# Smaller expert blocks in two mixture-of-experts layers: 48 rows in place of 64, and 22 overflow blocks in place of 16

## What is computed

```python
def hier_moe(h, w_grp, b_grp, w_rt, b_rt, w_up, w_down):
    g_gate, g_idx = top_k(softmax(xt @ w_grp + b_grp), 1)      # one of 4 groups
    e_val, e_idx = top_k(the 8 logits of that group, 2)        # two experts of it
    gate = softmax(e_val) * g_gate
    expert = g_idx * 8 + e_idx                                 # 2 of 32 experts for each token
    for each expert e, its rows x:
        a, u = split(x @ w_up[e], 2)                           # w_up[e]   1024 x 1024
        y = (silu(a) * u) @ w_down[e]                          # w_down[e]  512 x 1024
    return the sum over a token's two experts of gate * y
h = h + hier_moe(...)        # output: h without the 16 learned tokens
```

```
18 21 22 31 22 33 18 39 | 25 40 28 36 12 14 22 31
38 30 54 42 47 42 54 53 | 27 41 25 33 25 31 39 31
```

## Time and profile before

| | |
|---|---|
| median of 3 runs | 2815.74 us |
| profiled execution, its own time | 2807.85 us |
| its span | 2806.0 us |
| TensorE busy | 2567.0 us (91%) |
| weight loads into TensorE | 1356.2 us (48%) |
| VectorE, ScalarE, GpSimd busy | 875.4, 568.4, 480.3 us |
| HBM read and written | 507.26 MB, 23.10 MB |

### The profile page before, as it was taken

One profiled execution on the slowest core, in us unless ns is written; L12 is line 12 of the kernel. 1 busy time (PEld: TensorE's weight loads), 2 busy tenths in 40 slices (PEclk: granted clock), 3 DMA queues, 4 the chain that ended last, 5 costly groups with the idle time before them and its releaser, 6 DMA issues. The chain is left out here.

```text
span 2806.0 us, 37484 instructions
## 1 busy us (share of the span) xinstructions
PE 2567.0 (91%) x15258; PEld 1356.2 (48%) x15258; DVE 875.4 (31%) x1809; ACT 568.4 (20%) x1341; POOL 480.3 (17%) x682
## 2 busy tenths in 40 slices
PE   7997898988989999889999999959999899989985
PEld 4654444435554454555555555434455454444442
DVE  2306512353251221664111211120556542111112
ACT  2106112232221111631000010021345111000000
POOL 2623210071231121340000000020344200000001
PEclk9998999997999999999999999979999899999997
DMA  5211013110021420125999999951001089999997
GB/s 177 85 66 46 30 35 120 42 41 2 4 77 37 144 90 32 38 77 209 358 411 411 411 411 411 369 193 53 32 32 61 1 337 411 411 411 411 411 411 282
DMA packets 180273, 532.33 MB, mean 190 GB/s; under 512 B 21360, under 2 KB 31472, under 8 KB 180144
## 3 DMA queue, kind: packets, MB, share of 16 engines
q1 hardware_dynamic: 167536, 505.22, 46.5%
q10 hardware_dynamic: 10240, 16.79, 1.6%
q0 software_dynamic: 2368, 8.52, 0.9%
HBM read 507.26 MB, written 23.10 MB: 189 GB/s over the span
## 5 line engine op out<-in xcount | busy, mean ns | idle before, releaser
L344 PE MATMUL psum<-weight_ring,hidden_T 128*128 128x512 f32 (+2 forms) x1216 | 475.9, 548 | 2.7 <-PEq L576 1.6
L344 PEld LDWEIGHTS psum<-weight_ring,hidden_T 128*128 128x128 f32 x1216 | 228.7, 191 | 223.0 <-issue 158.2
L2982 PE MATMUL psum<-arena,hidden_T 128*64 128x512 f32 x1344 | 296.2, 592 | 0.0
L2971 PEld LDWEIGHTS psum<-hidden_T,arena 128*128 128x128 f32 x2304 | 266.8, 192 | 49.6 <-issue 49.6
L2971 PE MATMUL psum<-hidden_T,arena 128*128 128x128 f32 x2304 | 283.3, 278 | 0.0
L2994 PE MATMUL psum<-weight_ring,hidden_T 128*64 128x512 f32 x1024 | 235.4, 602 | 34.1 <-DMA weight_ring<-in_moe_w_down 30.0
L3248 POOL DMA_INDIRECT arena<-expert_rows_out,arena x18 | 20.4, 1133 | 1061.9 <-issue 534.3
L2982 PEld LDWEIGHTS psum<-arena,hidden_T 128*64 128x64 f32 x1344 | 100.5, 137 | 186.9 <-issue 186.9
L2982 PE MATMUL psum<-weight_ring,hidden_T 128*64 128x512 f32 x704 | 155.0, 592 | 0.0
L2994 PEld LDWEIGHTS psum<-weight_ring,hidden_T 128*64 128x64 f32 x1024 | 71.0, 137 | 153.0 <-issue 128.5
L2976 DVE TENSOR_TENSOR hidden_T<-psum,norm_gains 128x512 f32<-128x512 f32 x64 | 44.3, 691 | 293.9 <-PE psum L2982 182.7
(11 more groups left out here) (546 smaller groups left out, 3195.5 us busy)
## 6 DMA issues: line engine op xcount, KB each, us to landing
arena<-in_moe_w_up SPq DMA_DIRECT2D x84, 2048.0 KB, 24.1
weight_ring<-in_moe_w_down SPq DMA_DIRECT2D x64, 2048.0 KB, 24.0
weight_ring<-in_moe_w_up SPq DMA_DIRECT2D x44, 2048.0 KB, 23.4
weight_ring<-in_hg_w_in SPq DMA_DIRECT2D x8, 2048.0 KB, 10.6
weight_ring<-in_ev_w_in SPq DMA_DIRECT2D x8, 1536.0 KB, 6.9
weight_ring<-in_fox_w_in SPq DMA_DIRECT2D x6, 2048.0 KB, 8.1
weight_ring<-in_od_w_in SPq DMA_DIRECT2D x5, 2048.0 KB, 8.0
weight_ring<-in_ple_w_gate SPq DMA_DIRECT2D x4, 2048.0 KB, 9.3
```

Source lines behind the costliest of these rows:

```text
L344: last = nc.tensor.matmul(out, l, r, start=i == 0, stop=i == len(left) - 1)
L2971: last = nc.tensor.matmul(g.psum[:, c // 4, (c % 4) * P:(c % 4 + 1) * P], keep[:, i, c * P:(c + 1) * P], row[:, i, :], start=i == 0, stop= ...
L2982: last = nc.tensor.matmul(g.psum[64 * q:64 * q + 64, 2 + n, :].rearrange("p (s c) -> p s c", s=2), xT[:, k // 4, k % 4, ROWS * n:ROWS * n ...
```

## The change

Each expert's own block has 48 rows, a pair's slots are 96, and there are 22 overflow blocks of 48 rows. What follows from it: the 0/1 matrices, the moving side of `pick` and the copies of `place` have 96 columns for 128; the two stores of a result have 48 rows for 64; the block counts are taken against 10 multiples of 48 instead of 8 of 64; the table of overflow blocks is made with 22 x 32 comparisons instead of 16 x 32; the overflow loop goes around 22 times when there is any block. The products with w_up and w_down keep 64 columns of their stationary side. For the second expert of a pair that reaches 16 columns beyond the 96, so VectorE sets these to zero once per layer, with a wait, ahead of the first `place`. A scratch table moves to another buffer. The one DMA that zeroes the overflow rows early in the program covers 1056 rows instead of 1024.

```diff
-ROWS = 64
-OVER = 16
+ROWS = 48
+PAIR = 2 * ROWS
+OVER = 22
+BLOCKS = 11
@@ host_constants
-    c["steps"] = np.tile(ROWS * np.arange(1, 9, dtype=np.float64), (P, 1))
+    c["steps"] = np.tile(ROWS * np.arange(1, BLOCKS, dtype=np.float64), (P, 1))
@@ zero_expert_rows
-    rows = g.a["y_rows"][NEXP * ROWS:].rearrange("(p n) (two c) -> p (n two) c", p=P, c=512)
+    rows = g.a["y_rows"][NEXP * ROWS:].rearrange("(p n) (two c) -> p (n two) c", p=PAIR, c=512)
@@ stage_route
-            TT(bg, cnt.unsqueeze(2).to_broadcast([P, NEXP, 8]), g.c("steps")...
+            TT(bg, cnt.unsqueeze(2).to_broadcast([P, NEXP, BLOCKS - 1]), g.c("steps")...
@@ stage_experts
-    numbers = g.c("slots").unsqueeze(1).to_broadcast([P, T, P])
+    numbers = g.c("slots")[:, 0:PAIR].unsqueeze(1).to_broadcast([P, T, PAIR])
@@ pick
-                last = nc.tensor.matmul(g.psum[:, c // 4, (c % 4) * P:(c % 4 + 1) * P], keep[:, i, c * P:(c + 1) * P], row[:, i, :], ...
+                last = nc.tensor.matmul(g.psum[:, c // 4, (c % 4) * P:(c % 4) * P + PAIR], keep[:, i, c * P:(c + 1) * P], row[:, i, :], ...
@@ tensor_up
-                last = nc.tensor.matmul(..., xT[:, k // 4, k % 4, ROWS * n:ROWS * n + ROWS], wv[:, k, q, :, :], ...
+                last = nc.tensor.matmul(..., xT[:, k // 4, k % 4, ROWS * n:ROWS * n + 64], wv[:, k, q, :, :], ...
@@ store
-        a = eng.dma_start(rows[:, 0:512], y[n][0:64, :])
-        b = eng.dma_start(rows[:, 512:], y[n][64:128, :])
+        a = eng.dma_start(rows[:, 0:512], y[n][0:ROWS, :])
+        b = eng.dma_start(rows[:, 512:], y[n][64:64 + ROWS, :])
@@ VectorE in stage_experts
             gates_and_overflow(dve, late)
+            nc.vector.memset(xT[:, :, :, PAIR:PAIR + 16], 0.0).then_inc(*late.up())
+            dve.wait_ge(*late.last())
             for n in range(2):
                 dve.wait_ge(turned[n].sem, turned[n].base + 1)
                 place(n).then_inc(placed[n].sem, 1)
```

More of the change, by code:

```diff
@@ L322, in zero_expert_rows @@
     zeros = g.small[:, 512:1024].unsqueeze(1)
-    rows = g.a["y_rows"][NEXP * ROWS:].rearrange("(p n) (two c) -> p (n two) c", p=P, c=512)
-    sp.dma_start(rows, zeros.to_broadcast([P, OVER * ROWS // P * 2, 512])).then_inc(*g.y_rows_zeroed.up(16))
+    rows = g.a["y_rows"][NEXP * ROWS:].rearrange("(p n) (two c) -> p (n two) c", p=PAIR, c=512)
+    sp.dma_start(rows, zeros[0:PAIR].to_broadcast([PAIR, OVER * ROWS // PAIR * 2, 512])).then_inc(*g.y_rows_zeroed.up(16))
 def inverse_root(g, pool, out, sums, scale, chain, done, times=None):
@@ L2679, in stage_route @@
     ovb, inc, base, obase = (g.take(NEXP) for _ in range(4))
-    big = turned_logits.rearrange("p t n -> p (t n)")[:, 0:OVER * NEXP]
+    big = g.hT.rearrange("p k t -> p (k t)")[:, 2 * len(TILES) * NEXP:(2 * len(TILES) + OVER) * NEXP]
     t1 = g.hT.rearrange("p k t -> p (k t)")[:, 0:2 * T * NEXP].rearrange("p (a t e) -> p a t e", a=2, t=T)
@@ L2883, in _ @@
             dve.wait_ge(*counts_ready.at(2))
-            bg = big[:, 0:NEXP * 8].rearrange("p (e j) -> p e j", e=NEXP)
-            TT(bg, cnt.unsqueeze(2).to_broadcast([P, NEXP, 8]), g.c("steps").unsqueeze(1).to_broadcast([P, NEXP, 8]), ALU.is_gt).then_inc(*chain.up())
+            bg = big[:, 0:NEXP * (BLOCKS - 1)].rearrange("p (e j) -> p e j", e=NEXP)
+            TT(bg, cnt.unsqueeze(2).to_broadcast([P, NEXP, BLOCKS - 1]), g.c("steps").unsqueeze(1).to_broadcast([P, NEXP, BLOCKS - 1]), ALU.is_gt).then_inc(*chain.up())
             TT(t1, OH, twice(C), ALU.mult).then_inc(*chain.up())
@@ L2950, in stage_experts @@
     xT = flat[:, 0:2 * 512].rearrange("p (a k r) -> p a k r", a=2, k=4)
-    row, match0, match1 = (flat[:, 1024 + 640 * n:1024 + 640 * n + T * P].rearrange("p (t r) -> p t r", t=T) for n in range(3))
+    row, match0, match1 = (flat[:, 1024 + 640 * n:1024 + 640 * n + T * PAIR].rearrange("p (t r) -> p t r", t=T) for n in range(3))
     s, act_, aT = flat[:, 2944:3200], flat[:, 3200:3456], flat[:, 3456:3712].rearrange("p (j r) -> p j r", j=2)
@@ L2955, in stage_experts @@
     yr = g.a["y_rows"]
-    numbers = g.c("slots").unsqueeze(1).to_broadcast([P, T, P])
-    of = [slot[:, k, 0:T].unsqueeze(2).to_broadcast([P, T, P]) for k in range(2)]
+    numbers = g.c("slots")[:, 0:PAIR].unsqueeze(1).to_broadcast([P, T, PAIR])
+    of = [slot[:, k, 0:T].unsqueeze(2).to_broadcast([P, T, PAIR]) for k in range(2)]
     def match(k, out):
@@ L2970, in pick @@
             for i in range(T):
-                last = nc.tensor.matmul(g.psum[:, c // 4, (c % 4) * P:(c % 4 + 1) * P], keep[:, i, c * P:(c + 1) * P], row[:, i, :], start=i == 0, stop=i == T - 1)
+                last = nc.tensor.matmul(g.psum[:, c // 4, (c % 4) * P:(c % 4) * P + PAIR], keep[:, i, c * P:(c + 1) * P], row[:, i, :], start=i == 0, stop=i == T - 1)
         return last
     def place(a):
-        return nc.vector.tensor_tensor(xT[:, a, :, :], g.psum[:, a, :].rearrange("p (k r) -> p k r", k=4), gain[:, 4 * a:4 * a + 4].unsqueeze(2).to_broadcast([P, 4, P]), ALU.mult)
+        return nc.vector.tensor_tensor(xT[:, a, :, 0:PAIR], g.psum[:, a, :].rearrange("p (k r) -> p k r", k=4)[:, :, 0:PAIR], gain[:, 4 * a:4 * a + 4].unsqueeze(2).to_broadcast([P, 4, PAIR]), ALU.mult)
     def tensor_up(n, b, half):
@@ L2981, in tensor_up @@
             for q in range(2):
-                last = nc.tensor.matmul(g.psum[64 * q:64 * q + 64, 2 + n, :].rearrange("p (s c) -> p s c", s=2), xT[:, k // 4, k % 4, ROWS * n:ROWS * n + ROWS], wv[:, k, q, :, :], start=k == 0, stop=k == KD - 1)
+                last = nc.tensor.matmul(g.psum[64 * q:64 * q + 64, 2 + n, :].rearrange("p (s c) -> p s c", s=2), xT[:, k // 4, k % 4, ROWS * n:ROWS * n + 64], wv[:, k, q, :, :], start=k == 0, stop=k == KD - 1)
         return last
```

## The result

The change makes the kernel slower: 2899.57 us (median of 4 runs) against 2816.45 us for the kernel before on the same chip, a ratio of 1.0294 with an interval of [1.0267, 1.0322]. 2911 us was predicted, 11.4 us too much. The profiled execution took 2895.06 us (its span is 2893.3 us), 87.2 us more than the one before, for which +95 was predicted.

What follows compares the result with a forecast made beforehand. DMA transfers at 411 GB/s were taken to bound layer 1, PE most of layer 0. Terms -7.1 + 0 + 0 + 96 + 6 = +95 us on 2815.7 gave 2911 us, 3.4% slower; range 2895 to 2930.

Steps and rivals of the forecast that it cites:

- The count: Overflow blocks needed with 48 rows: 0 in layer 0 and 3 in layer 1.
- (b): Overflow loop: no block runs, leaving 2808.6 us, faster by 0.25%; chance 0.05.
- (c): Overflow loop: another count, two or four blocks, 33 us less or more, 2878 or 2944 us; chance 0.07.
- Part 1: Both expert layers: smaller stores make transfers earlier, 4.6 us in layer 1 and 2.5 in layer 0, -7.1 us.
- Part 2: Pick products: 96 moving columns for 128 gain 0, since the stationary side sets the 0.112 us each.
- far bound of -6: Pick products in both layers: the gain in us if their time did scale with the moving columns.
- Part 3: Small VectorE edits, overflow table, memset and zeroing DMA: 0, bounds -0.5 and +2 us.
- Part 4: End of layer 1: three overflow blocks in a chain at 33 us each, 99 us, +96 after 3 not new.
- Part 5: Overflow loop after the blocks: 19 empty turns on ScalarE at 0.3 us, +6 us, bounds 2 and 12.
- Rival (a): Overflow blocks: PE stays at half clock throughout, 41.7 us a block, +123, 2939 us; chance 0.08.
- Rival (d): Overflow loop: each of 22 turns pays for fetching code, 2943 us at 2 us per turn; chance 0.06.
- The lowest case of the range: Whole kernel: 31 us per block, short empty turns and a scaled pick, given as 2898 us.

Runs made afterwards that it cites:

- store by count: Kernel before, 64-row blocks, always storing 48 rows of an expert and the last 16 only if it has more: 0.9983, and 0.9987 when run again.

## Why the prediction was right

The sign, the mechanism and the size held: three blocks at the end of layer 1, one behind the other, against a few us of smaller stores. Point by point:

- **The count.** Three blocks ran, all in layer 1. That rules out rivals (b) and (c).
- **Part 1, stores.** -7.1 predicted. The trace has -4.2 and -4.3, together -8.5. Layer 1's 4.3 is the term of 4.6. In layer 0, 2.5 was predicted as the point at which PE is late next, and PE itself came to be 0.05 us faster an expert, 1.5 us over 30: together 4.0 of the 4.2. The formula of bytes over 411 GB/s gave the right number for 48 rows, but not for the reason given, and that is luck: blocks of 56 rows have fewer bytes too, and of the 0.08 us an expert that the formula gives them they gain 0.02. With 64 and with 48 rows the share of the fullest engine and the bytes give the same number.
- **Part 2, pick.** A pick still takes 0.11 us. It is not quite nothing: 20 picks take 2.37 us for 2.40. Its far bound of -6 was well away. The rule of the Trainium skill, page "TensorE: Matmul & The Clock Gate", section "Back-to-back issue gap", by which a pick would have fallen to 43 ns, is not what this trace shows; the section itself says that the formula holds for a product in isolation and counts too little at few columns.
- **Part 3.** Nothing seen, within the -0.4 us left over.
- **Part 4, the blocks.** 33 us each were predicted, 31.3 measured in the second. By its terms, as the timeline above has them: issue of w_up to PE's start 13.4 for 14.65; w_up 8.78 for 8; silu to w_down 1.9 for 2.0; w_down 3.65 for 4.5; from there to the next issue 3.5 for 3.8. The half clock fell where it was expected in blocks 2 and 3, in the picks (9.9 and 9.7 us for 64, clock 0.68), under the cover of the load; in the first block the picks ran at full clock (7.38 us), and w_up bore 1.7 us of the low clock in each block, behind waits of 4.00, 1.96 and 1.80 us for the load; behind the 1.26 and 1.19 us of the two kernels with earlier loads it took 7.09 us, at full clock. w_down bore none, 0.85 us under its term. The largest miss of the part was the landing of w_up, 1.2 us sooner than its term; w_up itself, 0.8 above, made up for part of both. Together 93.45 us, less the 3.75 us that the old landing took ahead of the gathers (4.75 less the 1.0 us of the meeting): +89.7 us for +96.
- **Part 5, empty turns.** 6 us predicted from a guess of 0.3 us a turn; it is 0.44 us and 8.4 us in all. The branch itself was sized rightly from the earlier trace rows; what stands between branches, a register step and a move with the gaps around them, was not.
- **Rival (a)**, half clock throughout, would have needed 41.7 us a block. The picks of blocks 2 and 3 went part of the way, but w_up came back to a clock of 1.00 in its second half and w_down had it throughout. **Rival (d)** asked for 2 us a turn, and a turn took 0.44.
- **The lowest case of the range.** The 2898 given for it doesn't follow: 3 x 31 - 3 + 2 - 7.1 - 6 = +79 us makes 2895, which is the bound that stands beside it.

Of the 7.8 us between the predicted +95 and the profiled +87.2, about 6.3 lie in the blocks, 1.4 in the layers' loops, 1.9 in the last expert's wait and clock, and 0.4 in the rest of the program; the empty turns give 2.4 back. The medians are 83.1 us apart, 4 less than the two profiled executions; that is within what single executions scatter (2892.67 to 2904.25 us).

## What to carry to other kernels

A fallback that runs once per item at the end of a stage, with loads, products and stores in one chain, is priced by its chain and not by its rows: count how often the data calls it before making the main path's tile smaller. When a wait is taken from such a chain, ask what it had been covering; here the load covered the picks, so that removing its wait alone gained little, and the load in its new place held up the landing of the stores, which made the block 2 to 3 us longer. Moving the picks as well took 10 us off. And look at what a queue-issuing engine does just ahead of the last step: two store issues in front of one copy made PE stand 1.56 us longer here, and in one layer of two the pause was followed by the lower clock, for another 1.70 us.

## What the runs showed of the hardware

- A store of 56 rows gains next to nothing over one of 64, and one of 48 does (15.94, 15.95 and 15.80 us an expert). The store queue counts 70, 80 and 64 packets a store, 14, 16 and 16 more than rows.
- An empty loop turn costs 0.44 us on ScalarE; its two branches are 0.095 us of it.
- A store's landing grows from 2.0 to 6.0 us behind one 2 MB load that is issued 0.04 us ahead of the pair of stores.
- The same pause of about 2 us ahead of a w_down was followed by the lower clock level at one place and not at the other: 2.03 us by 5.35 in layer 1 and by 3.65 in layer 0 of the kernel before, 1.83 us by 3.66 in the kernel after, 1.77 us by 5.35 in layer 0 and by 3.65 in layer 1 of the kernel with loads earlier. All six longer ones, 2.69 to 3.90 in the kernels that store by count, were followed by 5.11 to 6.22. The first block's picks, behind a wait of 2.80 us, took 7.38 us in the changed kernel and 10.38 in the one with three more blocks, which has the same code there. What decides it stays open.
